# Opening stage of a two-layer encoder trunk: the identity table's load moves from SyncE's queue to ScalarE's

## The reference

```
x = x + mixer_i(rms_norm(x, norm_mix_g[i]))
x = x + (silu(h @ w_gate) * (h @ w_up)) @ w_down        # h = rms_norm(x, norm_ffn_g[i])
...
out = rms_norm(x, final_norm_g)
```

## Time and profile before

| | us |
|---|---|
| median of 3 runs | 1075.24 |
| lowest, highest | 1074.99, 1075.47 |
| the profiled execution, device time | 1075.9 |
| its span | 1073.9 |
| TensorE busy in the span | 1061.6 (99%) |
| VectorE, ScalarE, GpSimd busy | 801.9, 478.3, 226.4 |

### The profile page before, as it was taken

One profiled execution on the slowest core, in us unless ns is written; L12 is line 12 of the kernel. 1 busy time (PEld: TensorE's weight loads), 2 busy tenths in 40 slices (PEclk: granted clock), 3 DMA queues, 4 the chain that ended last, 5 costly groups with the idle time before them and its releaser, 6 DMA issues. The chain is left out here.

```text
span 1073.9 us, 18481 instructions
## 1 busy us (share of the span) xinstructions
PE 1061.6 (99%) x6600; PEld 942.1 (88%) x6600; DVE 801.9 (75%) x1099; ACT 478.3 (45%) x708; POOL 226.4 (21%) x212
## 2 busy tenths in 40 slices
PE   8999999999999999999999999999999999999997
PEld 7888888999999998888878766789999999978887
DVE  5755659999999999444455687599999999984343
ACT  6312236644444446222346777465444444542222
POOL 6000001323323320222110355013233233101110
PEclk9999999999999999999999999999999999999999
DMA  7323242232333233432436511113323323332321
GB/s 200 110 87 115 81 115 79 79 118 90 105 117 96 99 107 94 122 93 89 116 98 147 138 49 40 40 44 114 117 80 115 117 83 112 108 108 87 102 67 79
DMA packets 146807, 106.38 MB, mean 99 GB/s; under 512 B 4505, under 2 KB 142929, under 8 KB 146769
## 3 DMA queue, kind: packets, MB, share of 16 engines
q1 hardware_dynamic: 146240, 104.81, 32.3%
q0 software_dynamic: 496, 1.08, 0.3%
q10 hardware_dynamic: 32, 0.01, 0.0%
HBM read 99.58 MB, written 2.10 MB: 95 GB/s over the span
## 5 line engine op out<-in xcount | busy, mean ns | idle before, releaser
L386 PE MATMUL ps<-x_op_hi,op_w_hi 128*128 128x256 f32 x1232 | 349.1, 283 | 0.9 <-DVE op_w_lo L530 0.9
L387 PE MATMUL ps<-x_op_lo,op_w_hi 128*128 128x256 f32 x1232 | 348.6, 283 | 0.0
L388 PE MATMUL ps<-x_op_hi,op_w_lo 128*128 128x256 f32 x1232 | 348.6, 283 | 0.0
L386 PEld LDWEIGHTS ps<-x_op_hi,op_w_hi 128*128 128x128 f32 x1232 | 236.5, 192 | 2.7 <-DVE op_w_lo L530 1.5
L387 PEld LDWEIGHTS ps<-x_op_lo,op_w_hi 128*128 128x128 f32 x1232 | 236.5, 192 | 0.1
L388 PEld LDWEIGHTS ps<-x_op_hi,op_w_lo 128*128 128x128 f32 x1232 | 236.5, 192 | 0.0
L386 PE MATMUL ps<-hid_hi,wgt_hi 128*128 128x512 f32 (+1 forms) x542 | 208.5, 385 | 0.6 <-DVE hid_lo L1164 0.6
L370 DVE TENSOR_TENSOR wgt_lo<-raw,wgt_hi 128x1024 fp32r<-128x1024 f32 (+5 forms) x127 | 136.3, 1088 | 96.2 <-ACT wgt_hi L361 94.7
L388 PE MATMUL ps<-hid_hi,wgt_lo 128*128 128x512 f32 (+1 forms) x542 | 206.4, 381 | 0.0
L387 PE MATMUL ps<-hid_lo,wgt_hi 128*128 128x512 f32 (+1 forms) x542 | 206.4, 381 | 0.0
L361 ACT ACTIVATE wgt_hi<-raw 128x1024 fp32r<-128x1024 f32 (+5 forms) x127 | 105.6, 844 | 148.5 <-PE ps L388 140.9
(11 more groups left out here) (167 smaller groups left out, 1218.0 us busy)
## 6 DMA issues: line engine op xcount, KB each, us to landing
pair_raw<-in_ffn_w_gate SPq DMA_DIRECT2D x22, 1024.0 KB, 5.2
pair_raw<-in_ffn_w_up SPq DMA_DIRECT2D x22, 1024.0 KB, 5.2
raw<-in_conv_w_in SPq DMA_DIRECT2D x24, 512.0 KB, 3.7
raw<-in_ffn_w_down SPq DMA_DIRECT2D x32, 384.0 KB, 3.4
raw<-in_ffn_w_down SPq DMA_DIRECT2D x32, 320.0 KB, 2.8
raw<-in_conv_w_out SPq DMA_DIRECT2D x8, 512.0 KB, 3.5
raw<-in_mla_w_o SPq DMA_DIRECT2D x8, 512.0 KB, 3.8
x_nat<-in_x SPq DMA_DIRECT2D x4, 512.0 KB, 7.0
```

The lines of the kernel that those rows point to most:

```text
L386: nc.tensor.matmul(acc, wh, xh, start=first, stop=False)
L387: nc.tensor.matmul(acc, wh, xl, start=False, stop=False)
L388: return nc.tensor.matmul(acc, wl, xh, start=False, stop=last)
```

## The change

The identity's load leaves the head of SyncE's list, which then begins with x0, and is issued by ScalarE instead, right behind the mixer norm's weights. Everything else stays.

```diff
@@ -541,7 +541,6 @@
                 sp.dma_start(x_nat[:, :, c * n:(c + 1) * n],
                              x_dram.rearrange("(t p) d -> p t d", p=P)[:, :, c * n:(c + 1) * n]).then_inc(x_in[c], 16)
 
-            sp.dma_start(ident, consts[:, 0:P]).then_inc(ident_in, 16)
             load_x(0)
             load_unit(sp, "conv_in", 0, 0)
             load_x(1)
@@ -698,6 +697,7 @@
         def _(sc):
             sc.dma_start(gain_rows[0:2 * DC, :],
                          w["norm_mix_g"].rearrange("l (r c) -> (l r) c", c=P)).then_inc(mix_in, 16)
+            sc.dma_start(ident, consts[:, 0:P]).then_inc(ident_in, 16)
 
             def chunk(t, m):
                 return t[:, ds(m, 1), :].rearrange("p a s -> p (a s)")
```

## The result

| us | before | changed |
|---|---|---|
| median | 1075.47 (15 runs) | 1077.98 (15 runs) |
| lowest, highest | 1074.99, 1076.61 | 1076.3, 1078.49 |
| profiled execution, device time | 1075.9 | 1078.03 |
| its span | 1073.9 | 1076.0 |

The changed kernel is slower: the ratio is 1.0019, with a 95% interval of 1.0013 to 1.0026. That is 2.0 us by the ratio and 2.5 us by the medians. I had forecast 1075.0 and a range of 1074.2 to 1076.4. The result is outside it, on the side of rival C.

The account below looks back on a forecast made before the run. TensorE, busy 1061.6 of 1073.9 us, was taken as the bound, so only its standing still could change. The three parts, -0.25 + 0 + 0, took the median from 1075.24 to 1075.0, range 1074.2 to 1076.4.

Parts of the forecast that it names:

- rival C: TensorE's wait ahead of turn_gains: the identity lands late, past 4.7, and the time becomes 1076.1 to 1077.4; chance 0.12.
- Part 1: SyncE's queue loses its first entry: x0 is issued 0.44 us earlier, x2 lands 0.26 earlier, taken as 0.25.
- Part 2: ScalarE's queue gains the identity's issue, 0.39 to 0.43 us; its table load moves to 1.6, which costs nothing.
- Part 3: The identity lands later, ahead of turn_gains on TensorE: at 3.5 instead of 2.76, which costs nothing.
- The price of a late L: Identity landing at L: gain whole up to about 4.2, a loss past about 4.7, then one microsecond per microsecond.
- rival D: A gap at 3.44 delays TensorE's rise from 1.2 to 2.4 GHz; past 12.18 it costs 1.5 to 2 us, 1076.9; chance 0.04.
- The joint: TensorE asks for W1's lo part at 14.86, ready at 14.20: 0.66 us of cover before ScalarE's and VectorE's backlog costs time.

Follow-up runs that it names:

- two on-chip kernels: Changed kernel with the identity made on GpSimd instead of loaded, with keep_warm(5) or keep_warm(6): medians 1075.34 (before 1075.62) and 1075.18 (before 1075.55).
- mirror: Kernel before with the two small loads exchanged: SyncE issues the norm weights, then x0; ScalarE issues the identity alone. Median 1075.59, before 1075.55.
- less warm: Kernel before with keep_warm(1) instead of keep_warm(5) ahead of the waits, transfers as before: median 1075.83, before 1075.38, ratio 1.0001.
- changed kernel again: The changed kernel, unaltered, measured once more beside the others on one chip: median 1077.77, before 1075.55, ratio 1.0018.
- x1 ahead of W0: Changed kernel with x1 issued ahead of W0 on SyncE's queue: median 1077.53, before 1075.38, ratio 1.0016.
- swap: Changed kernel with the identity first and the norm weights second on ScalarE's queue: median 1077.62, before 1075.62, ratio 1.0019.
- bridge: Changed kernel with keep_warm(13) instead of keep_warm(5) ahead of the wait for the identity: median 1076.67, before 1075.62, ratio 1.0011.
- before, late turns: Kernel before with keep_warm(13) instead of keep_warm(5), transfers issued in the same order: median 1076.3, before 1075.55, ratio 1.0006.

## Why the prediction was wrong

**Part 1 points the right way, and its size isn't shown.** I put x2's earlier landing at 0.26 us, between 0 and 0.44. The two on-chip kernels turn x2 0.26 and 0.59 us earlier, the second outside my bounds. But kernels with the order of before differ too: x2 is turned at 12.18, 12.10 (mirror) and 12.37 (less warm). One trace each can't size a term of 0.26 us, and that one of them hits it is luck. Their medians, 0.37 and 0.28 us below before, fit it without excluding zero. In the changed kernel the gain is hidden: TensorE came to x2 at 14.15 and waited for nothing. One reading was mixed: the 1.15 us of standing before x2 is the weight load's, the matmul's own is 0.72 (2.3 less 1.6); nothing in the sum hangs on it.

**Part 2 was right.** ScalarE's table load moved to 1.79 (I said 1.6), and what is late on ScalarE behind it waited for TensorE, not for this.

**Part 3 failed, in one term: the landing of the identity.** I took L = 3.5 "nearer to the quiet rows", because x0's transfer itself ran at only 131 GB/s until 3.00. It was about 6.4. The slow filling of the engines was no room for the identity: rows of a transfer issued half a microsecond earlier on another queue went ahead of it, and some of the next one too. The bound from the other side, 5.6 to 6.9 from GpSimd's small loads, was the good one; it was measured beside the same big transfers. I had dismissed it as far away and of another kind of queue. That the load is what the two cases have in common is my reading; the runs show that the landing moves with what SyncE's queue carries (5.2, 4.7 and 3.7 us).

**The rule I leaned on does not carry it.** The Trainium skill, page "DMA: Bandwidth & Descriptors", section "Queues, rings and completion order", has a DMA engine go round the queues that have work; I had drawn from it that L would stay under 4. Between 3.40 and 4.25 SyncE's queue moved 436 packets and ScalarE's one. The rule would still stand if ScalarE's rows weren't there yet, or if an engine's turn at a queue were longer than I took it to be; no run tells. The other rule, that spreading saves issue time only (the Trainium skill, same page, section "Issuing engines are not separate DMA queues"), is not contradicted: in the two on-chip kernels x0 is issued 0.38 us earlier (0.82 for 1.20) and x2 turned 0.26 and 0.59 us earlier. The 0.21 us above the 0.38 are less than the 0.27 us between executions of one order (12.10 and 12.37).

**The price of a late L was right, and incomplete.** By my steps a landing at 6.42 costs 6.42 - 4.68 = 1.74 us. I had left the clock as rival D, a case of its own. It isn't one: the same wait that makes C makes the gap that makes D. From turn_gains to ScalarE's first chunk the kernel before takes 6.35 - 3.44 = 2.91 us, of which 0.30 is the wait for x0, so 2.61 us, with the lower clock up to about 5.0; the changed kernel takes 9.71 - 6.46 = 3.25, all at the lower clock. That adds 0.64. 1.74 + 0.64 = 2.38 us, and the statistic's matmul is 2.38 us later. About 0.3 us of it is regained up to the end of the span (2.1). D's own path was wrong: I had products at half rate past 12.18, but line 1492's matmuls were back at 275 ns by 10.5, before the first product at 12.65.

That both come to 2.38 is closer than the steps deserve, but their cover does hold. I had 0.28 + 0.66 = 0.94 us between ScalarE's backlog and TensorE. Taking ScalarE's first chunk from 6.35 and the statistic's matmul from 26.50, the two are late by:

| us late | first chunk | statistic's matmul | difference |
|---|---|---|---|
| changed kernel | 3.36 | 2.38 | 0.98 |
| changed kernel again | 3.33 | 2.41 | 0.92 |
| x1 ahead of W0 | 2.87 | 1.94 | 0.93 |
| swap | 2.44 | 1.47 | 0.97 |
| bridge | 2.36 | 1.42 | 0.94 |
| before, late turns | 2.36 | 1.39 | 0.97 |

The joint appeared at unit 1, where the steps said, but the first and longer wait was at unit 0 (0.62 us at 12.65), which they left out. And the start doesn't explain every median: swap and bridge reach the statistic within 0.05 us of each other, yet their medians are 0.95 us apart. Their profiled executions are no guide, being 0.6 below the one's median and 0.75 above the other's. That stays open.

**The chances.** C had 0.12 and D 0.04, as if apart. With L from the loaded rows, 5.6 to 6.9, and 0.64 us for the clock added, C alone would have given 1076.8 to 1078.1, and the range would have had to reach there.

## What to carry to other kernels

A small load that an engine needs early belongs ahead of the big ones in time of issue and first on its queue: there, either queue landed it in about 2 us (2.0 and 1.9). Moving it to another queue, second there and half a microsecond behind a 512 KB transfer, made 2.0 us of landing into 5.2. To price such a move, use the landing times of loads under the same load, not those of quiet ones. And a new wait of TensorE in its first microseconds is to be priced with the matmuls behind it at the lower clock.

## What I had not expected of the hardware

Two queues side by side didn't share evenly: for 0.85 us one of them moved 436 packets and the other, with 64 KB issued, one. The landing of one and the same 64 KB load on ScalarE's queue went from 1.9 us (small load beside it) to 3.0 (x0 issued with it), 3.7 (x0 issued 0.5 us before), 4.7 (x1 beside it as well) and 5.2 (W0, in rows half as long, beside it as well). In the first two it was first on its queue, in the others second. Even 8 KB went from 1.9 to 4.2 us when it came second.
